# Hawk-Conformer-MoE step: separate SBUF for the bias tables, loaded and split during the convolution

## The chip, the cores and the metric

The kernel runs on one core of a Trainium2 chip. The metric is the time of one execution on the device in microseconds. The core has five engines that run side by side, each with its own instruction queue, and that wait for each other through semaphores: TensorE (PE: matmuls and transposes), VectorE (DVE), ScalarE (ACT), GpSimd (POOL) and SyncE (SP, which here only issues DMAs). They work on SBUF and PSUM; DMA queues move data between HBM and SBUF.

## The reference, cut to what matters

One inference step of a one-layer decoder for 256 prompt tokens and 8 x 4 sample tokens (288 in all), model width 1024:

```python
hn = rmsnorm(x, g_mix)
z = hn @ w_in                       # xa | u_glu (2 x 1024) | gate_a | gate_b
xa_c = causal_dwconv(xa, ..., w_conv_a, b_conv_a)      # width 4
y_a = rglru(xa_c, ...)
v = u_glu[..., :D] * sigmoid(u_glu[..., D:])
v_c = causal_dwconv(v, ..., w_conf_dw, b_conf_dw)      # width 31
y_b = silu(layernorm(v_c, ...)) @ w_conf_pw + b_conf_pw
h = x + (sigmoid(gate_a) * y_a + sigmoid(gate_b) * y_b) @ w_out
# mixture of experts on rmsnorm(h, g_ffn): top 4 of 32
for e in range(32):
    g = minimum(xf @ w_gate[e] + b_gate[e], 7)
    u = clip(xf @ w_up[e] + b_up[e], -7, 7)
    hdn = (u + 1) * (g * sigmoid(1.702 * g))
    out += combine[:, e] * (hdn @ w_down[e] + b_down[e])
y = rmsnorm(h + out, g_final)
```

The 32 experts' weights (3 x 4 MB each) are read once. The change touches the three tables `b_gate`, `b_up` and `b_down`, 32 rows of 1024 float32 each.

## The kernel before, in words

The program has a mixer stage (all before the experts) and an expert stage. It is written with explicit waits, so each engine's order is the order of the code.

**Mixer.** The 1024 channels stand in 8 tiles of 128 partitions, each with 256 prompt columns and 32 sample columns. PE computes the products with `w_in` tile by tile (L846), ACT empties them, and POOL multiplies value and sigmoid for each tile (L519, L521). The width-31 convolution runs on DVE, two tiles at a time, in a loop of four turns over pairs of tiles: each turn has 31 taps on two tiles, the first tap of a turn as a tensor_scalar (L1348) and the others as scalar_tensor_tensor of 128x256 float32 with two tensor inputs in SBUF (L1351), 60 in a turn. The sample columns go another way: POOL multiplies them with all taps (L535, eight instructions for two tiles, written into `taps_s`), and half way through a turn, after the first 30 taps, DVE reduces them (L1335, L1339). That releases POOL to write the products for the next pair of tiles. So POOL is half a turn ahead of DVE. After the loop DVE starts the width-4 convolution (L1320, L1323) and subtracts the mean (L1357); POOL adds up the tiles (L563) for the mean, a matmul with ones on PE (L906), and then, from ACT's squares (L690), for the variance (L568, PE L911). Layer norm, the RG-LRU scan (L1393), the pointwise matmul (L928) and the merge (L1398, L1401) follow.

**From the merge to the first gather.** PE multiplies with `w_out` (L985 for the 32 sample tokens, L951 for the two prompt tiles); DVE adds the residual (L1410, L1415); ACT sums squares (L632); DVE scales (L1419). The normed rows `h_tok` are then cut into three bf16 parts, since the gather is a bf16 matmul with a 0/1 selection: ACT casts (L737), POOL subtracts the cast from the rest (L601, function `rest`), ACT casts again, twice per token tile, tiles in the order 2, 0, 1. PE turns the rows (L829) and computes router logits (L978), DVE takes the top four (L1435 to L1446), PE ranks the tokens (L1006), DVE writes the selection (L1474), and PE gathers the first expert's inputs (L1020, L1022). `keep_warm` (L959) are idle matmuls of PE on the identity.

**The bias tables.** A bias enters the experts' matmuls as a bf16 matmul whose weights pick three rows of a table: the float32 bias as three bf16 parts on partitions 0 to 95. `bias` is that table for gate, up and down. `load_bias(m)` (L575) issues three DMAs of 32 rows each from POOL's queue. `split_bias(m)` makes the parts on POOL: a cast (L583), a subtraction (L590), a cast, a subtraction, a cast, each waiting for the one before. Before the change `bias` and its raw rows lie in the work area `ws` on top of the mixer's tiles, so POOL waits for the merge (`s_m`), issues the loads, clears the unused rows (L606, and L607 for `h_rows`, the parts of the sample rows), and then splits between the calls of `rest`:

```python
                pool.wait_ge(s_m, NT)
                load_bias(0)
                load_bias(1)
                pool.memset(bias[3 * E:, :, :], 0.0)
                pool.memset(h_rows[3 * T_S:, :], 0.0)
                split_bias(0)
                pool.wait_ge(s_btab, 1)
                load_bias(2)
                rest(0, TILE_ORDER[0])
                split_bias(1)
                rest(1, TILE_ORDER[1])
                rest(2, TILE_ORDER[2])
                split_bias(2)
```

PE waits before the first gather for all h parts (`s_split`, 9 casts) and for the tables of gate and up (`s_btab` 2).

**Experts.** SP streams chunks of 2 MB into a ring of six slots; the chunk `m` waits until PE has used chunk `m-6` (`used`). The first of these waits stands behind PE's first chunk of expert products (L1042), after the first gather.

Of the kernel before, what the change touches and what calls it, by code (L numbers as in the profile page):

```python
# [22 lines left out]
BF16 = mybir.dt.bfloat16  # L23
# [3 lines left out]
P = 128  # L27
D = 1024
NT = D // P
# [8 lines left out]
E = 32  # L38
CAP = 64
# [55 lines left out]
def build(nc, A, O):  # L95
    with ExitStack() as ctx:
        def sb(name, shape, dt=F32):
            return ctx.enter_context(nc.sbuf_tensor(name, shape, dt))

        def sem(name):  # L100
            return ctx.enter_context(nc.semaphore(name))
# [13 lines left out]
        bias_rows = sb("bias_rows", [P, E], BF16)  # L115
        tri = sb("tri", [P, P], BF16)
# [19 lines left out]
        def take(words):  # L136
            at[0] += words
            assert at[0] <= WS, at
            return ws[:, at[0] - words:at[0]]
# [34 lines left out]
        stc_rows = ig_w[:, 0:2 * D].rearrange("p (h d) -> p h d", h=2)  # L174
        st_v = ga_w[:, TW:TW + 2 * D].rearrange("p (b d) -> p b d", b=2)
# [20 lines left out]
        x_e_w = take(2 * NT * CAP)  # L196
        x_e = x_e_w.rearrange("p (b k s) -> p b k s", b=2, k=NT)
# [4 lines left out]
        bias = take(3 * D // 2).bitcast(BF16).rearrange("p (m d) -> p m d", m=3)  # L202
        raw_bias = [y_e, x_e_w, y_e]
# [26 lines left out]
        s_btab = sem("bias_tables_ready")  # L230
        s_gfin = sem("g_final_loaded")
# [145 lines left out]
        with nc.Block() as block:  # L377
# [113 lines left out]
            def _(pool):  # L491
# [4 lines left out]
                pool.memset(ones_h[:], 1.0).then_inc(s_const, 1)  # L496
                pool.wait_ge(s_seed, 1)
# [12 lines left out]
                for name, r, n in (("w_conf_dw", W_DW, KC), ("w_conv_a", W_CA, KA), ("b_conv_a", B_CA, 1),  # L510
                                   ("b_rg_a", B_RA, 1), ("b_rg_x", B_RX, 1), ("rg_lambda", LAM, 1), ("b_conf_dw", B_DW, 1),
                                   ("g_conf_ln", G_LN, 1), ("b_conf_ln", B_LN, 1), ("b_conf_pw", B_PW, 1)):
                    pool.dma_start(par_rows[r:r + n, :], A[name][0] if n > 1 else A[name]).then_inc(s_par, 16)

                for c in range(0, NT, 2):
# [14 lines left out]
                    for cc in (c, c + 1):  # L530
                        pool.wait_ge(s_v, 2 * cc + 2)
                        v = vx[:, cc, HC + T_P:].rearrange("p (s t) -> p s t", s=SEQS)
                        w = par[:, cc, W_DW:W_DW + KC].unsqueeze(1).to_broadcast([P, SEQS, KC])
                        for t in range(STEPS):
                            ins = pool.tensor_tensor(taps_s[:, cc % 2, :, t, :], v[:, :, t:t + KC], w, ALU.mult)  # L535
                        ins.then_inc(s_tap, 1)

# [35 lines left out]
                def load_bias(m):  # L573
                    for r in range(3):
                        pool.dma_start(raw_bias[m][r * E:(r + 1) * E, :],  # L575
                                       A[("b_gate", "b_up", "b_down")[m]][0]).then_inc(s_bias[m], 16)

                def split_bias(m):

                    pool.wait_ge(s_bias[m], 48)  # L580
                    for s in range(3):
                        n = (3 - s) * E
                        ins = pool.tensor_copy(bias[0:n, m, :], raw_bias[m][0:n, :])  # L583
                        if s == 2:
                            ins.then_inc(s_btab, 1)
                            break
                        ins.then_inc(s_part, 1)
                        pool.wait_ge(s_part, 4 * m + 2 * s + 1)
                        n -= E
                        pool.tensor_tensor(raw_bias[m][0:n, :], raw_bias[m][0:n, :], bias[0:n, m, :],  # L590
                                           ALU.subtract).then_inc(s_part, 1)
                        pool.wait_ge(s_part, 4 * m + 2 * s + 2)

# [10 lines left out]
                load_bias(0)  # L604
                load_bias(1)
                pool.memset(bias[3 * E:, :, :], 0.0)  # L606
                pool.memset(h_rows[3 * T_S:, :], 0.0)  # L607
                split_bias(0)
                pool.wait_ge(s_btab, 1)
                load_bias(2)  # L610
                rest(0, TILE_ORDER[0])
                split_bias(1)
                rest(1, TILE_ORDER[1])
                rest(2, TILE_ORDER[2])
                split_bias(2)
# [5 lines left out]
            def _(act):  # L621
# [149 lines left out]
                act.wait_ge(s_btab, 3)  # L771
# [43 lines left out]
            def _(pe):  # L815
# [328 lines left out]
                pe.wait_ge(s_btab, 2)  # L1144
# [21 lines left out]
                pe.wait_ge(s_btab, 3)  # L1166
# [72 lines left out]
            def _(dve):  # L1239
# [157 lines left out]
                for c in range(NT):  # L1397
                    V.scalar_tensor_tensor(mt[:, c, :], full(f"pw{c}")[:, 0:T], par[:, c, B_PW:B_PW + 1], gate_b[:, c, :],  # L1398
                                           ALU.add, ALU.mult).then_inc(empt_v, 1)
                    dve.wait_ge(empt_v, EV(f"pw{c}"))  # L1400
                    V.tensor_tensor(mt[:, c, :], mt[:, c, :], gate_a[:, c, :], ALU.add).then_inc(s_m, 1)  # L1401
                gain = g_ffn[:, :].unsqueeze(2).to_broadcast([P, NT, P])
# [250 lines left out]
```

## Time and profile before

| | us |
|---|---|
| median of 3 runs | 1261.91 (1260.13 to 1262.08) |
| the profiled execution | 1262.29 |
| its span | 1260.2 |
| from the span's start to the first convolution tap on DVE | 40.6 |
| convolution loop on DVE | 40.6 to 168.6 |
| merge done | 244.6 |
| first gather on PE | 305.2 |
| first expert products on PE | 310.3 |

PE is busy 94% of the span, DVE 42%, ACT 14%, POOL 9%. From some 345 us to the end the DMA queues move 420 GB/s, the experts' weights. The stretches before that are told apart by which engine waits for which.

### The profile page before, as it was taken

To read this page: it belongs to the slowest core of one execution; us is meant where nothing else is said; L and a number is where in the kernel's file an instruction comes from. 1 tells how busy PE (TensorE), PEld (TensorE's weight loads), DVE (VectorE), ACT (ScalarE), POOL (GpSimd) and SP (SyncE) were. 2 spreads that over 40 slices of the span, in tenths; PEclk is the share of its full clock that TensorE was granted. 3 is DMA by queue.
4 is the path that set the end of the run, shared out by engine and by line. 5 is a ranking of instruction groups with operands and counts; after the bars stand their busy time and mean duration, and the time that the engine had idled before them with its cause. 6 is when DMAs were issued, how large, how long until landed. Compare 5 with 4: busy or idle time off the path is not lost.

```text
span 1260.2 us, 18031 instructions
## 1 busy us (share of the span) xinstructions
PE 1188.1 (94%) x6801; PEld 591.1 (47%) x6802; DVE 524.8 (42%) x1001; ACT 179.1 (14%) x325; POOL 109.4 (9%) x134
## 2 busy tenths in 40 slices
PE   6999959988999999999999999999999999999996
PEld 4777747646444444444444443434343443434532
DVE  2799996845233232322323233323232323223242
ACT  3211217113010101010110101010101010101102
POOL 2422430174000000000000000000000000000000
PEclk9999979988999999999999999999999999999999
DMA  9943403355999999999999999999999999999991
GB/s 290 337 158 134 167 30 143 117 188 186 388 411 422 421 420 422 422 422 422 422 422 421 422 422 421 423 422 422 422 422 422 422 423 421 422 422 420 422 415 48
DMA packets 84661, 440.34 MB, mean 349 GB/s; under 512 B 8079, under 2 KB 30735, under 8 KB 35715
## 3 DMA queue, kind: packets, MB, share of 16 engines
q1 hardware_dynamic: 83075, 436.71, 85.8%
q0 software_dynamic: 1408, 3.14, 0.8%
q8 instruction: 25, 0.41, 0.1%
q14 instruction: 9, 0.07, 0.0%
q10 hardware_dynamic: 144, 0.00, 0.0%
HBM read 438.24 MB, written 2.43 MB: 350 GB/s over the span
## 4 chain that ended last, share of the span: by engine, by line
PE 59%; DMA 18%; DVE 10%; issue 7%; ACT 3%; POOL 1%; DVEq 1%; SPq 0%; ACTq 0%; POOLq 0%
PE ps L1042 28%; DMA ring<-in_w_up 17%; PE ps L1101 12%; PE ps L1020 6%; PE ps L1126 5%; DVE ws L1351 4%; PE ps L829 3%; PE ps L1022 1%; DMA ws<-in_b_gate 1%; PE ps L846 1%; PE ps L1033 1%; DVEq L1350 1%; PE ps L1130 1%; DVE ws L1323 1%; PE ps L951 1%
## 5 line engine op out<-in xcount | busy, mean ns | idle before, releaser
L1042 PE MATMUL ps<-ring,ws 128*64 128x512 f32 x2032 | 455.5, 596 | 18.5 <-DMA ring<-in_w_up 18.1
L1042 PEld LDWEIGHTS ps<-ring,ws 128*64 128x64 f32 x2032 | 138.6, 137 | 306.5 <-issue 263.5
L1101 PE MATMUL ps<-ring,ws 128*64 128x512 f32 x992 | 220.3, 597 | 0.0
L1506 DVE TENSOR_SCALAR ws<-ps 64x1024 f32<-64x1024 f32 x32 | 38.9, 1216 | 294.6 <-PE ps L1042 294.6
L846 PE MATMUL ps<-ws,ring 128*128 128x288 f32 x640 | 160.6, 415 | 0.7 <-issue 0.7
L846 PEld LDWEIGHTS ps<-ws,ring 128*128 128x128 f32 x640 | 124.7, 195 | 35.6 <-issue 0.8
L1101 PEld LDWEIGHTS ps<-ring,ws 128*64 128x64 f32 x992 | 70.0, 138 | 128.6 <-issue 126.2
L1527 DVE TENSOR_TENSOR acc<-ps,acc 128x1024 f32<-128x1024 f32 x32 | 39.2, 1225 | 194.1 <-PE ps L1126 194.1
L1020 PE MATMUL ps<-ws 128*128 128x64 bf16 x1536 | 112.2, 226 | 3.6 <-DVE ws L1474 3.6
L1351 DVE SCALAR_TENSOR_TENSOR ws<-ws,par x240 | 113.6, 551 | 0.0
L1020 PEld LDWEIGHTS ps<-ws 128*128 128x128 bf16 x1536 | 108.8, 166 | 6.7 <-issue 4.7
L764 ACT COPY ws<-ps 64x512 f32<-64x512 f32 x64 | 37.1, 579 | 289.0 <-PE ps L1101 288.6
L829 PE MATMUL ps<-ident,ws 64*128 64x64 f32 (+9 forms) x424 | 61.6, 287 | 15.4 <-DVE ws L1277 10.0
L1493 DVE TENSOR_TENSOR ws<-ps,g_ffn_c 128x512 f32<-128x512 f32 x32 | 22.1, 692 | 122.0 <-PE ps L1022 122.0
L829 PEld LDWEIGHTS ps<-ident,ws 64*128 64x128 f32 (+9 forms) x424 | 49.5, 178 | 49.8 <-issue 47.1
L1126 PE MATMUL ps<-ws 128*128 128x512 f32 x128 | 63.2, 618 | 1.5 <-ACT ws L764 1.5
L745 ACT COPY ws<-ps 128x512 f32<-128x512 f32 x32 | 18.7, 586 | 300.7 <-PE ps L829 300.7
L1022 PE MATMUL ps<-ws 128*128 128x64 bf16 x256 | 57.8, 226 | 0.0
L1532 DVE TENSOR_TENSOR acc<-ps,acc 32x256 f32<-32x256 f32 x64 | 26.7, 418 | 43.9 <-PE ps L1130 43.2
L1022 PEld LDWEIGHTS ps<-ws 128*128 128x128 bf16 x256 | 42.6, 166 | 0.0
L1126 PEld LDWEIGHTS ps<-ws 128*128 128x128 f32 x128 | 21.8, 189 | 42.4 <-issue 42.4
L755 ACT COPY ws<-ps 128x384 f32<-128x384 f32 x16 | 7.7, 478 | 227.9 <-PE ps L829 227.9
(202 smaller groups left out, 758.7 us busy)
## 6 DMA issues: line engine op xcount, KB each, us to landing
ring<-in_w_gate SPq DMA_DIRECT2D x127, 1024.0 KB, 20.9
ring<-in_w_up SPq DMA_DIRECT2D x127, 1024.0 KB, 23.3
ring<-in_w_down SPq DMA_DIRECT2D x124, 1024.0 KB, 19.3
ring<-in_w_in SPq DMA_DIRECT2D x20, 1024.0 KB, 11.2
ring<-in_w_conf_pw SPq DMA_DIRECT2D x4, 1024.0 KB, 6.3
ring<-in_w_out SPq DMA_DIRECT2D x4, 1024.0 KB, 6.8
ws<-in_w_down SPq DMA_DIRECT2D x2, 1024.0 KB, 5.8
acc<-in_x_prompt SPq DMA_DIRECT2D x2, 512.0 KB, 4.0
```

The lines of the kernel that those rows point to most:

```text
L764: ins = act.copy(y_e[d * CAP:(d + 1) * CAP, h * 512:(h + 1) * 512], ps[h * CAP:(h + 1) * CAP, bk, :])
L829: return nc.tensor.transpose(dst, src, ident[0:k, 0:k])
L846: ins = nc.tensor.matmul(z[:, 0:T], w[:, k, i * P:(i + 1) * P], hn[:, k, :], start=(k == 0), stop=(k == NT - 1))
L1020: nc.tensor.matmul(z, h_split[:, s, i, t::NT], sel[:, b, i, :], start=(s == 0 and i == 0), stop=False)
L1022: ins = nc.tensor.matmul(z, h_rows[:, t::NT], sel[:, b, 2, :], start=False, stop=True)
L1042: ins = nc.tensor.matmul(ps[m * CAP:(m + 1) * CAP, bk + h, :], x_e[:, b, 2 * q + t, :], w[:, m, t, h * 512:(h + 1) * 512], start=False, st ...
L1101: ins = nc.tensor.matmul(ps[h * CAP:(h + 1) * CAP, bk, :], hid_t[:, b, k, :], w[:, h * 512:(h + 1) * 512], start=False, stop=(k == NT - 1))
L1126: ins = nc.tensor.matmul(ps[:, bk + h, :], sel_t[0:rows, i * P:(i + 1) * P], y_e[0:rows, h * 512:(h + 1) * 512], start=True, stop=True)
L1351: V.scalar_tensor_tensor(y, x, w, y, ALU.mult, ALU.add).then_inc(s_conv, 1)
L1506: V.tensor_scalar(g_e, pair_ps(0, k), LIMIT, None, ALU.min).then_inc(s_gc, 1)
L1527: ins = V.tensor_tensor(acc[:, i, :], ps[:, bk:bk + 2, :].rearrange("p h n -> p (h n)"), acc[:, i, :], ALU.add)
L1532: ins = V.tensor_tensor(a, ps[c * T_S:(c + 1) * T_S, bk, 0:256], a, ALU.add)
```

## The change

- `bias` becomes a tensor of its own in SBUF (128 x 3 x 1024 bf16), no longer laid over the mixer's tiles. POOL clears all of it near the start of the program, after `ones_h` and ahead of the steps on `ident` and `tri` and of the parameter loads.
- The raw rows of the tables lie in the area of `ig_w`, which is free during the convolution: gate and down in its first 1024 columns, up in the next.
- `load_bias(0)` and `load_bias(1)` stand on POOL after the tap products of the first pair of tiles; `split_bias(0)` and `load_bias(2)` after those of the second, `split_bias(1)` after the third, `split_bias(2)` after the fourth.
- After the merge POOL only runs the three calls of `rest`. The clearing of the unused rows of `h_rows` moves to DVE, with a semaphore `s_zrow` for which PE's first gather waits.
- PE waits for all three tables before the first gather. ACT's wait and PE's second wait for them are gone.
- The reserve for descriptors of POOL's DMAs is set to 8192 bytes.

```diff
@@ constants, POOL @@
                 pool.memset(ones_h[:], 1.0).then_inc(s_const, 1)
+                pool.memset(bias[:, :, :], 0.0)
                 pool.wait_ge(s_seed, 1)
@@ convolution loop, POOL @@
                         ins.then_inc(s_tap, 1)
+                    if c == 0:
+                        load_bias(0)
+                        load_bias(1)
+                    else:
+                        split_bias(c // 2 - 1)
+                    if c == 2:
+                        pool.wait_ge(s_btab, 1)
+                        load_bias(2)
@@ after the merge, POOL @@
                 pool.wait_ge(s_m, NT)
-                load_bias(0)
-                load_bias(1)
-                pool.memset(bias[3 * E:, :, :], 0.0)
-                pool.memset(h_rows[3 * T_S:, :], 0.0)
-                split_bias(0)
-                pool.wait_ge(s_btab, 1)
-                load_bias(2)
-                rest(0, TILE_ORDER[0])
-                split_bias(1)
-                rest(1, TILE_ORDER[1])
-                rest(2, TILE_ORDER[2])
-                split_bias(2)
+                for n, i in enumerate(TILE_ORDER):
+                    rest(n, i)
@@ after the merge, DVE @@
+                dve.wait_ge(s_m, NT)
+                V.memset(h_rows[3 * T_S:, :], 0.0).then_inc(s_zrow, 1)
@@ before the first gather, PE @@
                 pe.wait_ge(s_split, 3 * TILES)
-                pe.wait_ge(s_btab, 2)
+                pe.wait_ge(s_btab, 3)
+                pe.wait_ge(s_zrow, 1)
                 gather(0, 0)
@@ program @@
-    nc = bacc.Bacc("TRN2", target_bir_lowering=False, num_devices=1)
+    nc = bacc.Bacc("TRN2", target_bir_lowering=False, num_devices=1, dynamic_dma_scratch_size=8192)
```

On POOL, in the second turn of its loop (tiles 2 and 3), the tap products were followed by the products of the next pair of tiles:

```order
L535 TENSOR_TENSOR ws<-ws,par 128x8x31 [waits v_ready]
L535 TENSOR_TENSOR ws<-ws,par 128x8x31 x3
L519 TENSOR_TENSOR ws<-ws 128x256 [waits psum_emptied_by_scalar]
L521 TENSOR_TENSOR ws<-ws 128x8x4
L519 TENSOR_TENSOR ws<-ws 128x256 [waits psum_emptied_by_scalar]
L521 TENSOR_TENSOR ws<-ws 128x8x4
L535 TENSOR_TENSOR ws<-ws,par 128x8x31 [waits v_ready,conf_conv_steps]
```

Now, at the same place on POOL (L557 is the former L535, L541 the former L519):

```order
L557 TENSOR_TENSOR ws<-ws,par 128x8x31 x3
L526 CAST bias<-ws 96x1024 [waits gate_bias_loaded]
L533 TENSOR_TENSOR ws<-ws,bias 64x1024 [waits bias_parts_steps]
L526 CAST bias<-ws 64x1024 [waits bias_parts_steps]
L533 TENSOR_TENSOR ws<-ws,bias 32x1024 [waits bias_parts_steps]
L526 CAST bias<-ws 32x1024 [waits bias_parts_steps]
L518 DMA ws<-in_b_down 32x1024 [waits bias_tables_ready]
L518 DMA ws<-in_b_down 32x1024 x2
L541 TENSOR_TENSOR ws<-ws 128x256 [waits psum_emptied_by_scalar]
```

Five instructions of 1024 columns and three DMA issues have come between; the third and fourth turns get the same five without the DMAs.

On POOL after the merge, before: the first two subtractions of `rest` (L601) stood behind the loads, the clearing and the whole first split:

```order
L606 MEMSET ws 32x3072
L607 MEMSET ws 32x1024
L583 CAST ws<-ws 96x1024 [waits gate_bias_loaded]
L590 TENSOR_TENSOR ws<-ws 64x1024 [waits bias_parts_steps]
L583 CAST ws<-ws 64x1024 [waits bias_parts_steps]
L590 TENSOR_TENSOR ws<-ws 32x1024 [waits bias_parts_steps]
L583 CAST ws<-ws 32x1024 [waits bias_parts_steps]
L575 DMA ws<-in_b_down 32x1024 [waits bias_tables_ready]
L575 DMA ws<-in_b_down 32x1024 x2
L601 TENSOR_TENSOR ws<-ws 64x1024 [waits h_parts_cast,psum_filled]
```

And now, on POOL after the merge, from the last output DMA to the load of `g_final`:

```order
L601 DMA out<-ws 8x1024
L610 TENSOR_TENSOR ws<-ws 64x1024 [waits h_parts_cast,psum_filled,merged_ready]
L610 TENSOR_TENSOR ws<-ws 32x1024 [waits h_parts_cast]
L610 TENSOR_TENSOR ws<-ws 128x1024 [waits h_parts_cast,psum_filled]
L610 TENSOR_TENSOR ws<-ws 128x1024 [waits h_parts_cast]
L610 TENSOR_TENSOR ws<-ws 128x1024 [waits h_parts_cast,psum_filled]
L610 TENSOR_TENSOR ws<-ws 128x1024 [waits h_parts_cast]
L616 DMA ws<-in_g_final 128x1024 [waits psum_filled]
```

Nothing but the six subtractions is left there.

## Rows read from the trace of the kernel before

**Rows 1.** Chain of waits (start us, us, engine and line)

```profile
267.88 2.14 POOL ws L601
```

**Rows 2.** Waits of PE over the span (us in total, times, longest)

```profile
PE ps L1042 <- DMA ring<-in_w_up: 18.1, 17, 1.3
PE ps L906 <- POOL ws L563: 15.8, 1, 15.8
```

**Rows 3.** Timeline, PE, 265 to 311 us (start us, us, instruction, count, [idle before <-releaser])

```profile
265.26 7.11 PE L951 MATMUL ps<-ring,ws 128*128 128x512 f32 x16
277.23 1.94 PE L829 MATMUL ps<-ident,ws 128*128 128x128 f32 x8 [4.85 <-DVE lg L1435]
278.96 8.42 PE L951 MATMUL ps<-ring,ws 128*128 128x512 f32 x16
...
298.71 2.83 PE L959 MATMUL ps<-ident 128*128 128x128 f32 x12
305.17 0.55 PE L1020 MATMUL ps<-ws 128*128 128x64 bf16 x6 [3.63 <-DVE ws L1474]
```

**Rows 4.** Timeline, POOL, 252 to 304 us

```profile
252.60 0.95 POOL L607 MEMSET ws<- 32x1024 bf16 x1
...
303.93 1.04 POOL L583 CAST ws<-ws 32x1024 bf16<-32x1024 f32 x1
```

**Rows 5.** Timeline, DVE, 252 to 306 us

```profile
252.16 1.94 DVE L1419 TENSOR_SCALAR ws<-acc,stat 128x1024 f32<-128x1024 f32 x1
...
263.76 0.69 DVE L1415 TENSOR_TENSOR acc<-ps,acc 128x512 f32<-128x512 f32 x1 [6.03 <-PE ps L951]
...
289.95 0.75 DVE L1419 TENSOR_SCALAR ws<-acc,stat 128x1024 f32<-128x1024 f32 x1
...
299.19 1.45 DVE L1466 TENSOR_SCALAR rank<-rank 128x96 f32<-128x96 f32 x1
...
301.92 3.10 DVE L1474 TENSOR_SCALAR ws<-slot_no,rank 128x64 bf16<-128x64 f32 x3
...
305.05 0.57 DVE L1474 TENSOR_SCALAR ws<-slot_no,rank 128x64 bf16<-128x64 f32 x3
```

**Rows 6.** Timeline, DVE: tap runs of turn 1 (second half), 2 and 4 (first half)

```profile
58.18 17.05 DVE L1351 SCALAR_TENSOR_TENSOR ws<-ws,par  x32
...
76.24 11.17 DVE L1351 SCALAR_TENSOR_TENSOR ws<-ws,par  x28
...
139.51 13.86 DVE L1351 SCALAR_TENSOR_TENSOR ws<-ws,par  x28
```

**Rows 7.** Windows of POOL (stretch, us, busy us (count), clock, DMA share, GB/s)

```profile
76.24:87.41 11.17, 0.00 (x0) 1.00 0.17 48
...
58.18:75.23 17.05, 9.28 (x12) 1.00 0.69 222
```

**Rows 8.** Timeline, POOL: a product beside an idle DVE, sums beside the taps

```profile
28.46 0.63 POOL L519 TENSOR_TENSOR ws<-ws 128x256 f32<-128x256 f32 x1 [20.01 <-ACT ws L660]
...
139.71 4.67 POOL L563 TENSOR_TENSOR ws<-ws 128x288 f32<-128x288 f32 x5
```

**Rows 9.** Lines by form, POOL: groups of the split (busy us, mean ns | idle before)

```profile
L590 POOL TENSOR_TENSOR ws<-ws 64x1024 f32<-64x1024 f32 x3 | 6.3, 2115 | 0.2
...
L583 POOL CAST ws<-ws 96x1024 bf16<-96x1024 f32 x3 | 3.1, 1030 | 4.9 <-DMA ws<-in_b_gate 4.9
...
L606 POOL MEMSET ws<- 32x3072 bf16 x1 | 2.7, 2653 | 0.0
```

**Rows 10.** Timeline, SP's DMA issues, 235 to 330 us

```profile
313.96 0.33 SPq L426 DMA_DIRECT2D ring<-in_w_gate  x1
```

**Rows 11.** Timeline, all engines, 0 to 12 us

```profile
1.08 0.91 DVE L1253 MEMSET acc<- 128x1024 f32 x1 [0.96 <-PEq L1643]
...
2.02 0.34 SPq L384 DMA_DIRECT2D acc<-in_x_sample  x1
...
7.27 1.04 ACT L632 ACTIVATE ws<-acc 128x1024 f32<-128x1024 f32 x1
```

## What the change does to the time, told before it was run

> **What bounds the kernel now.** PE is busy 94% of the span, so a share tells little; I went stage by stage and asked what ends last. From the first expert products on, PE and the weight stream pass the bound between them: all of PE's waits for weights there come to 18.1 us [rows 2]. That stage begins with the first gather. The chunk that starts the lasting stream is issued at 313.96, behind PE's first chunk of products [rows 10]. Whatever moves the first gather moves all behind it by as much, so the question is when the gather starts: 305.17 now [rows 3].
>
> Two stretches before it matter. After the merge, the chain goes through the load of `b_gate` and POOL's splitting, and reaches `rest` only at 267.88 [rows 1]. Before that, DVE's convolution is the bound: from 40.6 to 168.6 us DVE runs taps, turn after turn, and PE then stands 15.8 us waiting for the last sums [rows 2]. PE, ACT and POOL have room there; DVE has none. So the change takes work out of one stretch that is on the path and puts it on POOL beside another one that is on the path, and all depends on whether DVE feels it.
>
> **What is gained after the merge.** (a) `rest` for tile 2 no longer waits for the split. It needs the turned rows, there at about 256.9, so it starts 11 us earlier than 267.88. Then other work is late: the next square on ACT needs PE's `out01`, and the DVE addition after that starts at 263.76 and takes 0.69 [rows 5]. From there the chain takes square, root and scaling, by an estimate 2.6 us, so tile 0 is normed at about 267, with 5 us to spare: PE is in L951 until 272.4, and turns at once instead of at 277.23 after a wait of 4.85 [rows 3]: 4.9 us. L951 behind the turn takes 7.1, as the one at 265.26 does, instead of 8.42 [rows 3], since PE no longer stands still ahead of it: 1.3 us; and for the turn of 1.94 itself I take 0.8 off for the same reason, an estimate. Together **7.0 us**.
>
> (b) At the end of the stretch DVE is held up by POOL. The first selection (three tensor_scalar of 64 columns) takes 3.10 us from 301.92, and the same three take 0.57 at 305.05; the first ends at 305.02, within 0.1 us of the end of POOL's last cast at 304.97 [rows 4, 5]. The split of `down` behind `rest` holds three steps on mask and ranks ahead of it as well, the longest of them 1.45 us for 96 columns [rows 5], 3.0 us in all by my estimate. Without it the selection would be ready 5.5 us earlier relative to PE's last logits. The idle matmuls ahead of the gather are then the last: they end 298.71 + 2.83 = 301.54 now [rows 3], and start 0.8 us earlier and run mostly at the higher clock. I take **5.2 us**, between 3.9 (as long as now) and 5.5.
>
> (c) DVE's new clearing of `h_rows` costs nothing: DVE stands 4.0 us after the merge waiting for PE's first residual, and POOL's clearing of the same rows took 0.95 [rows 4]. If that cover were gone it would cost up to 0.9. POOL's clearing no longer holds DVE's scaling at 252.16, which takes 1.94 beside it and 0.75 alone [rows 5]; PE's `out00` hides that, so I count nothing. Gain in all 7.0 + 5.2 = **12.2 us**, bounds 10.9 and 12.9.
>
> **What is paid in the convolution.** POOL gets 15 more instructions of 1024 columns: 9 casts of 1.03 and 6 subtractions of 2.12 us [rows 9], 9.3 + 12.7 = 22.0 us. All fall in second halves of DVE's turns 1 to 3. POOL itself has room: it is half a turn ahead (about 16 us), and a split with its loads takes about 10.5 at this pace. PE waits longer for the new columns (some 20 us where it had nothing to do later but wait 15.8), and still has its five products done before the sums are.
>
> What DVE feels is read from its taps. With POOL idle, 28 taps take 11.17 us, 0.40 each [rows 6, 7]. Beside five of POOL's sums of 288 columns they take 13.86 [rows 6, 8]: 2.69 more, 0.54 for each. In the second half of turn 1, 32 taps take 17.05 instead of 12.77: 4.28 more, beside 12 instructions of POOL, eight of 248, two of 256 and two of 32 columns [rows 6, 7]. At 0.41 to 0.43 for each of the ten long ones that is it. A product of 256 columns alone takes 0.63 [rows 8], one of 288 would take 0.69. So each instruction of POOL costs DVE its own duration less 0.15 to 0.2, at every size that the trace has. By this rule a subtraction costs 1.92 and a cast 0.83: 6 x 1.92 + 9 x 0.83 = 11.5 + 7.5 = **19.0 us**; with 0.15 it is 19.7. The trace has no 1024-column instruction of POOL beside such a tap, so this goes four times beyond the longest row. The nearest rows at that length are DVE's operations on one SBUF input, which wait out POOL's whole instructions: the scaling at 252.16 ends 0.55 us after POOL's clearing has ended at 253.55 [rows 4, 5]. This is why I take the full length.
>
> The Trainium skill, SBUF — State Buffer, "SBUF: two separate sides", has a rule that speaks against this change: VectorE and GpSimd share a port pair under an exclusive lock, held for the whole instruction, against a VectorE operation in a two-port mode or with two SBUF inputs. By that rule the price is the 19 us; by a split of the bandwidth, which the page denies, it would be the 14.3 of the second rival. The rows on short instructions agree with either.
>
> **At the start.** POOL's clearing covers 3072 columns, 2.65 us [rows 9], ahead of `ident` and the parameter loads. `ident` is then ready at about 5.5, PE needs it at 10. The parameters land 2.65 later, which moves SP's second chunk from 13.9 to 16.6; PE needs it at 38. Nothing. But DVE's first clearing (1.08, 0.91 us) is such an operation as waits for POOL, and SP's load of the sample tokens at 2.02 waits for it [rows 11]. It could start only at about 4, so that load goes out at 4.6. It now lands by 6.7, behind the prompt; at 4.6 the queues are free of that, and by an estimate it takes 2.8 us and is there at 7.4, against ACT's third square at 7.27 [rows 11]. I take **0.3 us**, bounds 0 and 2.1 (if it takes as long again).
>
> **The DMAs.** Moved loads: 1.2 MB, at 420 GB/s some 3 us of all queues, beside a w_in stream that is tens of us ahead of PE. Nine issues of 0.5 us on POOL fall into its room. The second reserve of descriptors is halved or so; I have no row for a full one and count nothing, with up to 5 us of POOL's room as the bound.
>
> **Sum.** 19.0 + 0.3 - 12.2 = +7.1 us on the profiled execution of 1262.3, so 1269.4 there; the median of the runs is 0.4 lower, **1269.0**.
>
> **Rivals.**
> - *The forecast*, POOL's instructions hold the taps for their full length: 17.5 to 20.5, plus 0 to 2.1, less 12.9 to 10.9: +4.6 to +11.7, 1266.5 to 1273.6. Chance 0.70.
> - *Turns.* Both engines take every other slot while they collide. A tap streams 256 columns, 0.27 of its 0.40 us. It then takes 0.67, in which POOL gets 0.27 + 0.13 = 0.40 done, so each us of POOL costs 0.65: 22.0 x 0.65 = 14.3, sum +2.4, 1264.3. For it: the rows up to 288 columns fit it within 0.1. Against: the one-input rows above. Chance 0.10.
> - *Casts pass.* Only instructions of POOL with two inputs hold the taps: 11.5, sum -0.4, 1261.5. For it: all the rows beside taps that I count are products and sums. Against: even a clearing, which reads nothing, holds DVE's scaling [rows 4, 5]. Chance 0.06.
> - *The hold is per instruction, not per length* (the other side: faster). DVE loses one slot of arbitration, about 0.5 us, for each of POOL's instructions however long: 15 x 0.5 = 7.5, sum -4.4, 1257.5. For it: the trace shows only 0.41 to 0.54 at each. Against: the three sizes rise with length, 0.41, 0.43, 0.54. It decides from a mean hold under 0.8 us (12.2 / 15). Chance 0.07.
> - *The convolution is hidden*, or the order of POOL shifts so that the splits fall elsewhere: -11.9, 1250.0. Against it stands PE's wait of 15.8 for the sums [rows 2]. Chance 0.02.
> - *A starved POOL* (descriptors, or its half turn of lead used up), 5 us more than the forecast, near 1274. Chance 0.05.
>
> **How the numbers follow.** A measurement of this kernel can tell about 0.2%, 2.5 us, from no change. Slower by more: the forecast, the starved POOL and half of the turns, 0.80. Within: the other half and most of the casts, 0.10. Faster: 0.10. The range takes in the forecast and the turns: 1264 to 1273.6; widened to 1263.5.
>
> **What would show it.** Taps (L1351) whose longest instance is about 2.4 us instead of about 1, and second halves of turns 1 to 3 that are each about 6.3 us longer; POOL's subtractions beside them stretched little; PE's wait for L906 still there; PE turning tile 0 without a wait; the first selection in about 0.6 us. Measured from the merge to the first gather the time should fall from 60.5 to about 48.3 us, and from the start to the merge rise from 244.6 to about 264. It is wrong if the merge comes at about 252 (the per-instruction hold), or if the last third of the way to the gather keeps its 3.1 us selection.

## The result: 0.6% slower, as forecast

| | before | after |
|---|---|---|
| median of 5 runs, us | 1261.91 (1260.13 to 1262.96) | 1269.34 (1266.99 to 1271.23) |
| the profiled execution | 1262.29 | 1267.2 |
| start to first tap | 40.6 | 39.9 |
| convolution loop | 127.9 | 147.6 |
| loop end to merge | 76.1 | 76.1 |
| merge to first gather | 60.6 | 47.5 |
| first gather to first expert products | 5.1 | 4.9 |

The ratio of the medians is 1.0058, with an interval of 1.0045 to 1.0071. The forecast was 1269.0 in 1263.5 to 1273.6. The two profiled executions differ by 4.9 us, the medians by 7.4. The stages from the start to the first products (310.31 before, 315.99 after) come to +5.7 (-0.7 + 19.7 + 0.0 - 13.1 - 0.2, with rounding); what lies behind the first products took 0.8 us less in the profiled run of after. The five runs of this kernel lie up to 4.2 us apart, and the profiled one, 1267.2, is among the two shortest; where the others lose more was not followed.

The page of the kernel after, its span and busy times (us, share, instructions), and from section 5 the group of the taps (busy us, mean ns of one, idle time before):

```profile
span 1265.2 us, 18031 instructions
...
PE 1182.9 (93%) x6801; PEld 587.6 (46%) x6802; DVE 533.8 (42%) x1002; ACT 179.7 (14%) x325; POOL 109.6 (9%) x133
...
L1349 DVE SCALAR_TENSOR_TENSOR ws<-ws,par x240 | 133.8, 634 | 0.0
```

The shares hardly moved: PE 93% where it was 94%, POOL 9% as before. A reader who compares only them would see nothing of the 20 us lost and 13 won. The mean of a tap, 634 ns, hides it as well, since most taps are as short as ever. The view of this line's instructions shows minimum, median and maximum in ns:

```profile
L1349 DVE SCALAR_TENSOR_TENSOR ws<-ws,par x240: 471/479/2344, 40.9 to 187.1; - x120
```

The timeline of DVE after (start us, us, instruction, count) shows where the long ones are. Lines 1, 3, 4 are the second halves of turns 1 to 3; line 2 is the first half of turn 2, line 5 that of turn 4:

```profile
57.93 23.73 DVE L1349 SCALAR_TENSOR_TENSOR ws<-ws,par  x32
...
82.68 11.17 DVE L1349 SCALAR_TENSOR_TENSOR ws<-ws,par  x28
...
96.32 23.50 DVE L1349 SCALAR_TENSOR_TENSOR ws<-ws,par  x32
...
134.44 22.51 DVE L1349 SCALAR_TENSOR_TENSOR ws<-ws,par  x32
...
157.92 14.42 DVE L1349 SCALAR_TENSOR_TENSOR ws<-ws,par  x28
```

The first halves of turns 2 and 3, with POOL idle, are the 11.17 of [rows 6] to the hundredth. The second half of turn 1 went from 17.05 [rows 6] to 23.73, those of turns 2 and 3 from 16.98 and 16.56 to 23.50 and 22.51: 19.2 us in all. The rest of the 19.7 is in the first halves of turn 1 (14.08 to 14.55) and turn 4 (13.86 to 14.42), less 0.5 at turn 4's first tap. POOL stands beside them like this (timeline, POOL, the first split):

```profile
64.62 1.23 POOL L526 CAST bias<-ws 96x1024 bf16<-96x1024 f32 x1
65.93 2.18 POOL L533 TENSOR_TENSOR ws<-ws,bias 64x1024 f32<-64x1024 f32 x1
68.17 1.11 POOL L526 CAST bias<-ws 64x1024 bf16<-64x1024 f32 x1
69.37 2.18 POOL L533 TENSOR_TENSOR ws<-ws,bias 32x1024 f32<-32x1024 f32 x1
71.61 1.11 POOL L526 CAST bias<-ws 32x1024 bf16<-32x1024 f32 x1
...
275.55 2.12 POOL L610 TENSOR_TENSOR ws<-ws 64x1024 f32<-64x1024 f32 x1 [9.53 <-PE ps L827]
...
306.59 2.12 POOL L610 TENSOR_TENSOR ws<-ws 128x1024 f32<-128x1024 f32 x1 [1.16 <-ACT ws L736]
```

POOL's five take the lengths of [rows 9] plus 0.06 to 0.2: POOL is hardly stretched, DVE bears it all. The last two lines are the first and last subtraction of `rest` after the merge, alone with what they wait for: PE's turn and ACT's cast.

After the merge, PE (timeline; 283.82 is the product ahead of the turn of tile 0, which stands at 265.26 in [rows 3]):

```profile
283.82 7.11 PE L949 MATMUL ps<-ring,ws 128*128 128x512 f32 x16
290.77 1.05 PE L827 MATMUL ps<-ident,ws 128*128 128x128 f32 x8
291.65 7.03 PE L949 MATMUL ps<-ring,ws 128*128 128x512 f32 x16
...
309.26 1.58 PE L957 MATMUL ps<-ident 128*128 128x128 f32 x12
311.10 0.54 PE L1018 MATMUL ps<-ws 128*128 128x64 bf16 x6 [0.26 <-DVE ws L1474]
```

The turn has no wait before it, where 4.85 stood; the gather waits 0.26 where it waited 3.63. DVE in the same stretch (timeline; the scaling of tile 0, one step on the ranks, the first selection):

```profile
284.84 0.75 DVE L1419 TENSOR_SCALAR ws<-acc,stat 128x1024 f32<-128x1024 f32 x1
...
309.74 0.21 DVE L1466 TENSOR_SCALAR rank<-rank 128x96 f32<-128x96 f32 x1
...
310.37 0.58 DVE L1474 TENSOR_SCALAR ws<-slot_no,rank 128x64 bf16<-128x64 f32 x3
```

The scaling is through 5.2 us before PE turns; the selection is 0.58 instead of 3.10, the step on the ranks 0.21 instead of 1.45 [rows 5]. And PE's waits (us in all, times, longest), which answer to [rows 2]:

```profile
PE ps L827 <- issue: 19.7, 1, 19.7
PE ps L1040 <- DMA ring<-in_w_up: 19.4, 19, 1.3
PE ps L904 <- POOL ws L593: 14.1, 1, 14.1
```

The wait for the last sums of the convolution is still there, 14.1 after 15.8: the loop is still the bound of its stretch, so what it lost is lost. For the new 19.7 us the view names no releaser; they end at 150.82, 0.1 us after POOL's two copies of new columns, which stand behind the last split. Since PE then still waits 14.1 for the sums, they cost nothing by themselves.

### The profile page after: what moved, and what is told of

It reads as the page before. It is cut to its first block, busy times and chain, and to the rows that moved or that the text cites. A ratio compares the mean times of both kernels' runs of the same rounds, so it can differ in the third digit from the quotient of the medians.

```text
span 1265.2 us, 18031 instructions
## 1 busy us (share of the span) xinstructions
PE 1182.9 (93%) x6801; PEld 587.6 (46%) x6802; DVE 533.8 (42%) x1002; ACT 179.7 (14%) x325; POOL 109.6 (9%) x133
## 4 chain that ended last, share of the span: by engine, by line
PE 59%; DMA 19%; DVE 9%; issue 8%; ACT 2%; DVEq 1%; SPq 0%; POOL 0%; ACTq 0%; POOLq 0%
PE ps L1040 27%; DMA ring<-in_w_up 19%; PE ps L1099 12%; PE ps L1018 5%; PE ps L1124 5%; DVE ws L1349 4%; PE ps L827 3%; PE ps L949 2%; PE ps L1020 1%; PE ps L844 1%; PE ps L1031 1%; DVEq L1348 1%; PE ps L1128 1%; DVE ws L1321 1%; PE ps L1092 1%
## 5 line engine op out<-in xcount | busy, mean ns | idle before, releaser
L1040 PE MATMUL ps<-ring,ws 128*64 128x512 f32 x2032 | 455.7, 595 | 19.7 <-DMA ring<-in_w_up 19.4
L1349 DVE SCALAR_TENSOR_TENSOR ws<-ws,par x240 | 133.8, 634 | 0.0
L827 PE MATMUL ps<-ident,ws 64*128 64x64 f32 (+9 forms) x424 | 62.1, 288 | 30.1 <-issue 19.7
L1124 PEld LDWEIGHTS ps<-ws 128*128 128x128 f32 x128 | 21.8, 189 | 42.5 <-issue 42.5
## 6 DMA issues: line engine op xcount, KB each, us to landing
ring<-in_w_down SPq DMA_DIRECT2D x124, 1024.0 KB, 19.7
```

The costliest lines, as they stand in the source:

```text
L827: return nc.tensor.transpose(dst, src, ident[0:k, 0:k])
L1040: ins = nc.tensor.matmul(ps[m * CAP:(m + 1) * CAP, bk + h, :], x_e[:, b, 2 * q + t, :], w[:, m, t, h * 512:(h + 1) * 512], start=False, st ...
L1124: ins = nc.tensor.matmul(ps[:, bk + h, :], sel_t[0:rows, i * P:(i + 1) * P], y_e[0:rows, h * 512:(h + 1) * 512], start=True, stop=True)
L1349: V.scalar_tensor_tensor(y, x, w, y, ALU.mult, ALU.add).then_inc(s_conv, 1)
```

## The experiments

The theory: the loss is POOL's arithmetic alone, one instruction after the other, each holding DVE's taps for its length less 0.15 to 0.2 us; the gain after the merge is two things that can be had without that price. Rivals: shared slots, casts that pass, a hold per instruction, or a loss that comes from the loads and the changed order and not from the arithmetic. Ratios are against the kernel before, run on the same chip beside them (its medians: 1261.27, 1261.82 and 1261.47 us). Stages (us, from the profiled executions):

| kernel | loop | loop end to merge | merge to gather | longest tap | median |
|---|---|---|---|---|---|
| before | 127.9 | 76.1 | 60.6 | 1.02 | 1261.9 |
| a_again | 147.5 | 76.1 | 47.5 | 2.34 | 1269.4 |
| c_none | 128.2 | 76.1 | 47.5 | 1.23 | 1248.9 |
| c_casts | 136.5 | 77.8 | 47.5 | 2.07 | 1258.4 |
| c_subs | 140.1 | 77.8 | 47.5 | 2.34 | 1261.9 |
| b_late | 127.9 | 76.1 | 55.1 | 1.02 | 1257.2 |
| v_slots | 127.9 | 76.1 | 47.5 | 1.02 | 1250.9 |
| v_slots2 | 127.9 | 76.1 | 47.5 | 1.01 | 1249.1 |
| v_clear | 127.9 | 76.1 | 47.5 | 1.02 | 1251.0 |
| c_clears | 125.3 | 76.1 | 47.5 | 1.02 | 1245.4 |
| c_clear1 | 129.3 | 77.8 | 47.5 | 1.75 | 1251.5 |

### The change once more

No edit: the kernel after.

> The changed kernel once more, nothing edited. Its profiled run was 4.9 us above that of before, its median of five 7.4 us above. Theory (the sum: +19.7 in the convolution, -13.0 from merge to gather): a new profile again shows these two terms within 0.3 us, and the time is +5.5 to +9 us on before. Rival (the terms themselves scatter from run to run): the convolution loop differs from 147.6 us by over 1 us, or the stretch from merge to first gather from 47.5 by over 1 us.

Ratio 1.0062 [1.0049, 1.0075], all stages within 0.2 us of the first profile. The result stands.

### The change without the splitting

```diff
@@ split_bias(m) of the kernel after @@
                     pool.wait_ge(s_bias[m], 48)
-                    for s in range(3):
-                    ...
+                    pool.memset(bias[:, m, 0:2], 0.0).then_inc(s_btab, 1)
```

> The changed kernel with the arithmetic of the three splits left out (no casts, no subtractions; the bias tables stay zero, so the biases are not added); loads, the early clearing and everything after the merge as in the changed kernel. Theory (the full-length hold of DVE's taps is the whole loss): the convolution loop takes 127.5 to 128.5 us as before, the merge-to-gather stretch keeps its 47.5, and the time is 12 to 14 us below before, some 1249. Rival (the loads from POOL's queue or the early clearing cost something too): the loop stays 2 us or more above 128, or the first tap comes later than 41, and the time is above 1251.

Ratio 0.9905 [0.9891, 0.9920]; the loop takes 128.2. This kernel keeps the loads, their nine issues and the waits of POOL for them, and leaves out the parts of the bias. What it keeps comes to 0.3 us; the other 19.3 of the 19.7 us are the fifteen instructions. DVE's second halves of turns 1 and 2 (timeline):

```profile
58.15 17.37 DVE L1338 SCALAR_TENSOR_TENSOR ws<-ws,par  x32
...
90.17 16.99 DVE L1338 SCALAR_TENSOR_TENSOR ws<-ws,par  x32
```

### Casts alone, and subtractions alone

Casts alone (the subtractions left out):

```diff
@@ split_bias(m) of the kernel after @@
                         ins.then_inc(s_part, 1)
-                        pool.wait_ge(s_part, 4 * m + 2 * s + 1)
-                        n -= E
-                        pool.tensor_tensor(raw_bias[m][0:n, :], raw_bias[m][0:n, :], bias[0:n, m, :],
-                                           ALU.subtract).then_inc(s_part, 1)
-                        pool.wait_ge(s_part, 4 * m + 2 * s + 2)
+                        pool.wait_ge(s_part, 2 * m + s + 1)
```

> The changed kernel with the six subtractions of the splits left out, the nine casts kept (the bias tables then hold the rounded bias three times over, so biases are wrong). Theory (a cast, with one input and one output in SBUF, holds a tap for its duration less 0.15 to 0.2): 9 x 0.83 to 0.88, the convolution loop is 7.5 to 8 us above 127.9, time 5 us below before, some 1257. Rival (only two-input instructions of POOL hold the taps): the loop is at 128 to 129 us, time some 1249.

Subtractions alone (the casts left out):

```diff
@@ split_bias(m) of the kernel after @@
-                    for s in range(3):
-                        n = (3 - s) * E
-                        ins = pool.tensor_copy(bias[0:n, m, :], raw_bias[m][0:n, :])
-                        ...
+                    for s in range(2):
+                        n = (2 - s) * E
+                        pool.tensor_tensor(raw_bias[m][0:n, :], raw_bias[m][0:n, :], bias[0:n, m, :],
+                                           ALU.subtract).then_inc(s_part, 1)
+                        pool.wait_ge(s_part, 2 * m + s + 1)
+                    pool.memset(bias[:, m, 0:2], 0.0).then_inc(s_btab, 1)
```

> The changed kernel with the nine casts left out and the six subtractions kept (a clearing of 2 columns stands in for the last step; the tables stay zero, so biases are not added). Theory: 6 x 1.92 to 1.97 = 11.5 to 11.8 us, the convolution loop at about 139.5, time 1 us below before, some 1261. Rival (a long subtraction and the taps share by turns, and the rest of the loss came from the casts): 8 us or less, loop below 136.

c_casts: 0.9973 [0.9964, 0.9983]. c_subs: 1.0003 [0.9994, 1.0013]. The timeline of DVE in c_casts (turns 1 and 2), then that in c_subs (turn 1):

```profile
58.32 20.13 DVE L1345 SCALAR_TENSOR_TENSOR ws<-ws,par  x32
...
93.10 19.77 DVE L1345 SCALAR_TENSOR_TENSOR ws<-ws,par  x32
```

```profile
58.03 21.20 DVE L1343 SCALAR_TENSOR_TENSOR ws<-ws,par  x32
```

Against the 17.37 of c_none three casts add 2.76, 0.92 each, and two subtractions 3.83, 1.92 each. Over the whole loop it is (136.5 - 128.2) / 9 = 0.92 for a cast of 1.03 us and (140.1 - 128.2) / 6 = 1.97 for a subtraction of 2.12 (from the unrounded times). By loop or by turn, both are the instruction's length less 0.1 to 0.2. That settles it against three rivals: casts that pass would add nothing, a hold per instruction would give a cast and a subtraction the same price, and shared slots would give 0.67 and 1.38. The parts alone add up to 8.3 + 11.8 = 20.1, together they cost 19.3.

In both kernels loop end to merge rose by 1.7 us as well, which no expectation had; their medians are 1.2 us further above that of c_none than their loops say, their ratios 0.3 to 0.6 us. The timeline of PE in c_casts shows it, with the granted clock in windows (stretch, us, PE busy us (count), clock as a share of 2.4 GHz, DMA share, GB/s) below; the last fence has PE's matmuls ahead of the same wait in c_none:

```profile
179.94 12.78 PE L840 MATMUL ps<-ws,ring 128*128 128x288 f32 x48
194.85 0.72 PE L905 MATMUL ps<-ws,ones 128*128 128x288 f32 x2 [2.14 <-POOL ws L594]
195.41 17.37 PE L840 MATMUL ps<-ws,ring 128*128 128x288 f32 x64
```

```profile
193.00:195.00 2.00, 0.15 (x1) 1.00 0.63 164
195.00:197.00 2.00, 2.00 (x6) 0.64 0.99 418
197.00:199.00 2.00, 2.00 (x5) 0.51 1.03 438
199.00:205.00 6.00, 6.00 (x26) 1.00 0.04 12
```

```profile
171.47 13.56 PE L833 MATMUL ps<-ws,ring 128*128 128x288 f32 x48
```

PE waited 2.14 us for the variance sum, and the clock stood at the lower of its two levels, 1.2 GHz, from about 195.5 to 199; the 64 matmuls took 17.37 us. In c_none the wait was 1.36 and the same 64 took 15.68. In the kernels before and after it was 1.0. The sum itself is no later: the matmul that uses it starts 16.0 us after the one for the mean in c_casts (178.82 to 194.85) as in c_none (170.35 to 186.40). PE is only done sooner with the 48 matmuls between them, 12.78 us instead of 13.56 in c_none and 13.95 before, since the clock behind the mean's matmul is back at 2.4 GHz by about 182 (PE began at 178.82), in c_none only at about 175 (PE began at 170.35). c_subs and c_clear1 are alike: 12.67 and 12.82 for the 48, then waits of 2.25 and 2.11. So PE gains under 1 us ahead of the wait and loses 1.7 behind it. Why the clock comes back sooner in these three is open.

### The kernel before, with the last split behind the gather

```diff
@@ the kernel before, POOL after the merge @@
                 rest(2, TILE_ORDER[2])
+                pool.wait_ge(s_xg, 1)
                 split_bias(2)
```

> The kernel before with one part of the gain alone: the split of the down table waits until the first gather is done, so it no longer runs beside DVE's ranks and first selection; tables, areas and loads stay where they were. Theory (that split alone holds DVE, term b of the sum): the first selection takes 0.6 instead of 3.1 us, the first gather starts 5.0 to 5.6 us earlier, the time is 5 us below before, some 1257. Rival (the hold comes from the subtraction of the last token tile, or the idle matmuls end last as before): 0 to 2.5 us, 1260 to 1262.

Ratio 0.9969 [0.9957, 0.9981]: 3.9 us faster with one line. From the merge to the gather it is 55.1 instead of 60.6. DVE's first selection (timeline of DVE):

```profile
298.40 0.58 DVE L1475 TENSOR_SCALAR ws<-slot_no,rank 128x64 bf16<-128x64 f32 x3
```

It comes at 298.4, and POOL's first cast of that split at 302.74. So part (b) of the gain, put at 5.2, is 5.4, measured alone: from the end of the last product with `w_out` to the gather it is 12.6 instead of 18.0. The part up to that end is nearly untouched here (42.5 for 42.6), so the two are separate, and the rest of the 13.05 is (a).

### All of the gain, without the price

The splits go to places where POOL is idle and DVE has nothing of the path: gate behind the variance sums, up between the calls of `rest`, down behind the first gather.

```diff
@@ from the kernel after; raw rows in the areas of hn_w (gate), x_e_w (up), y_e (down) @@
-                    if c == 0:
-                        load_bias(0)
-                        load_bias(1)
-                    else:
-                        split_bias(c // 2 - 1)
-                    if c == 2:
-                        ...
@@ POOL behind the variance sums @@
+                pool.wait_ge(filled, JOB["gb7"] + 1)
+                load_bias(0)
+                split_bias(0)
@@ POOL after the merge @@
                 pool.wait_ge(s_m, NT)
-                for n, i in enumerate(TILE_ORDER):
-                    rest(n, i)
+                load_bias(1)
+                load_bias(2)
+                rest(0, TILE_ORDER[0])
+                split_bias(1)
+                rest(1, TILE_ORDER[1])
+                rest(2, TILE_ORDER[2])
+                pool.wait_ge(s_xg, 1)
+                split_bias(2)
```

PE again waits for two tables ahead of the first gather and for the third behind it, and ACT has its wait back, as in the kernel before.

> The changed kernel, but with the three splits in stretches where POOL is idle and DVE is idle or has room: gate after the last use of the normed input (its raw rows lie there), beside ACT's exponentials; up between the subtractions of token tile 2 and of tile 0; down behind the first gather. Raw rows of up and down lie where they did before the change. Theory: the convolution loop is back at 128 us and the stretch from merge to first gather stays at 47.5, so 1249 to 1250, 12 to 13.5 us below before. Rival (the split only moves its hold to other operations of DVE on the path, such as the product ahead of the scan or the scaling of tile 0): the loss shows up between the loop's end and the merge (76.1 us now) or in the merge-to-gather stretch, 3 to 7 us, so 1253 to 1257.

> The version with the splits in free slots once more, beside the one with the moved clearing: stages as in its first profile (loop 127.9, merge to gather 47.5), time 11 to 12.5 us below before.

Ratios 0.9917 [0.9902, 0.9931] and, once more, 0.9906 [0.9892, 0.9920]: 10 to 12 us faster than the kernel before, about 19 faster than the change. The loop is back at 127.9 and the gather stays at 47.5 after the merge: the same 22 us of arithmetic on POOL lengthened no stage here. The first median lies 2 us above that of c_none, the second with it. The timeline of POOL and the one of DVE show the only meeting with a long instruction of DVE:

```profile
210.59 1.03 POOL L528 CAST bias<-ws 64x1024 bf16<-64x1024 f32 x1
211.70 4.32 POOL L535 TENSOR_TENSOR ws<-ws,bias 32x1024 f32<-32x1024 f32 x1
```

```profile
211.47 2.57 DVE L1382 TENSOR_TENSOR ws<-ws 128x2304 f32<-128x2304 f32 x1 [4.36 <-ACT ws L709]
```

DVE's instruction began first and took its 2.57; POOL's subtraction took 4.32 instead of 2.12: 2.2 more, and until DVE ends at 214.04 there are 2.34. So the hold works both ways, and here whoever came second waited.

### Clearings in place of the arithmetic

Do instructions of POOL that only write hold the taps? First, five clearings of the same width where each split's five instructions stood:

```diff
@@ split_bias(m) of the kernel after @@
-                        ins = pool.tensor_copy(bias[0:n, m, :], raw_bias[m][0:n, :])
-                        ...
+                    for s in range(5):
+                        ins = pool.memset(bias[0:3 * E, m, :], 0.0)
+                        ...
```

> The changed kernel with each split's five steps replaced by five clearings of the same table, 96 x 1024 bf16, about 0.95 us each: POOL writes SBUF but reads nothing (tables stay zero, so biases are not added). Theory A (any instruction of POOL holds the taps): 15 x 0.75 = 11 us, loop at 139, time some 1260. Theory B (what is held is the reading side, so clearings pass beside taps with two inputs, as DVE's own clearing at the start passed beside POOL's of 2.67 us): loop at 128 to 129, time some 1249.

Ratio 0.9869 [0.9853, 0.9885], the fastest kernel of all, although it leaves nothing out of the loop that c_none has. DVE (turn 2), then POOL beside it (timelines):

```profile
90.75 16.14 DVE L1344 SCALAR_TENSOR_TENSOR ws<-ws,par  x32
```

```profile
97.45 4.96 POOL L525 MEMSET bias<- 96x1024 bf16 x5
102.38 5.01 POOL L536 TENSOR_TENSOR ws<-ws 128x256 f32<-128x256 f32 x1
107.35 0.30 POOL L538 TENSOR_TENSOR ws<-ws 128x32 f32<-128x32 f32 x1
```

Five clearings of 0.99 run beside the taps, and the taps take less than the 16.99 of c_none. What is new is the product of 256 columns behind them: 5.01 us for 0.65 to 0.9. It ends at 107.4, just after DVE's run of taps has ended at 106.9. Now it is POOL that is kept out, for a whole row of taps. DVE's run is 0.85 shorter than in c_none, and the first tap of turn 3 behind it 0.55 longer (1.36 for 0.81). Half of the 2.9 us by which this loop is shorter than that of c_none stands in turn 4, where POOL's five sums of 288 columns come late (148.32, 6.62 us) and are kept out too: the first half takes 11.17 for 13.85, the second 13.83 for 12.76.

The Trainium skill, SBUF — State Buffer, "SBUF: two separate sides", says that the lock works against a VectorE operation with two SBUF inputs only where GpSimd's operation reads SBUF. The trace agrees for the clearings, which the taps did not feel.

To see whether a single clearing does this to the product, in the fast version the clearing of `bias` near the start moved into the loop, one table per turn (v_clear), and in the kernel after one clearing took each split's place (c_clear1):

```diff
@@ v_clear, from v_slots @@
-                pool.memset(bias[:, :, :], 0.0)
...
                         ins.then_inc(s_tap, 1)
+                    if c:
+                        pool.memset(bias[:, c // 2 - 1, :], 0.0).then_inc(s_part, 1)
```

> The version with the splits in free slots, with the clearing of the bias tables moved from the start into the convolution: one table (128 x 1024 bf16) after the tap products of turns 2, 3 and 4 on POOL. With five such clearings (96 rows) in each turn the convolution loop had come out at 125.3 us, 3.0 below the 128.3 without them, because POOL's products of 256 columns behind them waited for a gap of DVE (3.2 and 5.0 us instead of 0.65 and 0.78) and DVE's taps ran at full pace meanwhile. Theory A (one clearing is enough to bring POOL's next reading instruction behind DVE): loop at 125.3 to 126.5, time 1.5 to 2.5 us below the version without it, some 1248.5. Theory B (it took five in a row, or was a matter of when they ended): loop at 127.9, same time as that version.

```diff
@@ c_clear1, split_bias(m) of the kernel after @@
                     pool.wait_ge(s_bias[m], 48)
-                    for s in range(3):
-                    ...
+                    pool.memset(bias[0:3 * E, m, :], 0.0).then_inc(s_btab, 1)
```

> The changed kernel with each split's five steps replaced by one clearing of 96 x 1024 bf16 (tables stay zero, so biases are not added); with five clearings the loop took 125.3 us, with only 2 columns cleared 128.3. Theory A (one long write-only instruction is enough): the products or the copy behind it last over 2 us and the loop is at 125.3 to 126.5. Theory B: loop at 128, products of 0.65 to 0.9 us.

v_clear: 0.9923 [0.9909, 0.9938], c_clear1: 0.9918 [0.9903, 0.9933]. POOL in v_clear (timeline):

```profile
96.58 0.95 POOL L561 MEMSET bias<- 128x1024 bf16 x1
97.49 0.72 POOL L542 TENSOR_TENSOR ws<-ws 128x256 f32<-128x256 f32 x1
```

One clearing does not keep the product out, 0.72, and the loop is 127.9 and 129.3 (why c_clear1's is 1.0 above that of c_none, with a longest tap of 1.75, was not followed). So v_clear is no gain over v_slots. No kernel can use c_clears as it stands, since it wins by clearing a table that is then empty.

The clearings need not be the cause. In the kernel before, which has none in the loop, POOL (first) met the taps of turn 1's first half (second) like this:

```profile
54.77 1.52 POOL L519 TENSOR_TENSOR ws<-ws 128x256 f32<-128x256 f32 x1 [6.48 <-ACT ws L660]
```

```profile
41.62 14.08 DVE L1351 SCALAR_TENSOR_TENSOR ws<-ws,par  x28
```

The product took 1.52 for 0.63 and ended at 56.3, 0.6 after the run of taps; in the kernel after, the same product took 1.99. In all twelve profiles (before, after and the ten runs), every reading instruction of POOL that came 4.4 us or more after both POOL's last reading one and the start of the run of taps waited for the end of the run, 16 in all. Every one that came 4.2 us or less after one of the two got in beside the taps (the product at 70.29 before: 4.22 idle, 1.09 us). Five clearings fill 4.96 us, one fills 0.95. So the pause in POOL's reading may be what counts; no run had such a pause made on purpose, and this stays argued.

## Why the prediction was right, step by step

- **The price in the convolution**, 19.0 by the rule, bounds 17.5 to 20.5: 19.7, of which 19.3 belong to the fifteen instructions. The rule held four times beyond the longest row it was read from. Of its two constants, length less 0.15 was the better: it gives 19.7. Measured apart, a cast costs 0.92 (0.83 predicted) and a subtraction 1.97 (1.92). The second halves got 6.7, 6.5 and 6.0 longer for the 6.3 told, and the longest tap is 2.344 us for 2.4. The step that mattered was to go by instructions on one SBUF input that wait out POOL's whole length [rows 4, 5], and not by the rows up to 288 columns, which also fit shared slots. The row named for it was no model for the taps, though: the scaling at 252.16 waits for a clearing, and clearings do not hold taps (c_clears). The better row was the first selection, which ends with POOL's last cast. So the length was rightly read, from a pair of instructions that behaves otherwise.
- **(a) up to the last product with `w_out`**, 7.0: 7.7. From the start of L951 to the turn it is 6.95 instead of 11.97 (5.0, told 4.9), the turn 0.88 instead of 1.73 (0.85, told 0.8), L951 behind it 7.03 instead of 8.42 (1.4, told 1.3), and PE reaches that L951 0.4 us earlier after the merge, which was not in the sum.
- **(b) the last third of the way**, 5.2: 5.4 in the kernel after, 5.4 alone in b_late. Parts (a) and (b) together, 13.05, lie just above the bounds that were told, 10.9 to 12.9. The gather now waits 0.26 for the selection: the idle matmuls, told to be last, end at 310.84, the first selection at 310.95.
- **(c) DVE's clearing of `h_rows`** costs nothing: it takes 0.48 at 263.75, and DVE waits 3.35 behind it for PE.
- **The start**, +0.3: this step had a wrong mechanism. The rows of after (timeline, all engines):

```profile
1.08 0.91 DVE L1251 MEMSET acc<- 128x1024 f32 x1 [0.95 <-PEq L1643]
...
1.35 2.67 POOL L497 MEMSET bias<- 128x3072 bf16 x1
...
2.02 0.34 SPq L384 DMA_DIRECT2D acc<-in_x_sample  x1
...
2.23 0.07 DVE L1254 MEMSET lg<- 128x12 f32 x1
```

  DVE's clearing did not wait for POOL's, nor did its small ones that began in the middle of it; the sample load went out at 2.02 as before [rows 11]. The step took a clearing for an operation like the scaling at 252.16, which has an SBUF input and did wait. The price of this is 0, not 0.3. The first tap comes between 39.9 and 41.3 in all the runs, in no order with the edits, which is more than the step was about.
- **The experts** start 5.9 us later in the trace (gather 305.17, now 311.10), the first chunk of the lasting stream 5.7 later, and PE's waits for weights are 19.4 for 18.1: all behind the gather moved with it, as told.

The sum by measured terms is 19.67 - 13.05 = +6.6 us, for +7.1 told and +7.4 between the medians. Each of the two large terms was told 0.7 to 0.9 us too small, and these two errors cancel almost wholly. That the sum is so near is luck in part; with either error alone it would still have been inside the range. What lies between the +6.6 and the +7.4 is not in the sum: the start (-0.7), the stretch to the first products (-0.2) and what lies behind them (-0.8) go the other way in the profiled runs, and the medians differ by 2.5 us more than these two runs.

Where the expectations of the experiments missed: c_casts (told 1257, 1258.4) and c_subs (told 1261, 1261.9), where the 1.7 us of the longer wait and the lower clock behind it were not expected; b_late (told 5 us below before, 3.9); v_slots (told 12 to 13.5 below before, 10.4 by its ratio, and 11.9 the second time), although its stages came as told; c_clears (told a loop of 128 and some 1249, 125.3 and 1245.4); v_clear, where theory A (1248.5) failed and the loop stayed at 127.9; c_clear1 (loop told at 128, 129.3).

## What to carry to other kernels

An idle share of POOL is no free room while DVE runs operations on two SBUF inputs back to back and is the bound: a reading instruction of POOL that gets in costs DVE nearly its full length, at all the lengths measured here, 248 to 1024 columns. Move such work to where DVE waits for another engine, and look for POOL's long instructions beside short DVE steps just ahead of a stage's end; here one wait of POOL gave 3.9 us, and the right places for all three splits gave 10 to 12. Before giving a busy stretch more work, look at what still waits for its end: the 15.8 us wait of PE said at once that nothing of the price would be hidden.

## What the runs showed of the hardware that was not expected

- The hold between POOL and DVE works in both directions: a subtraction of POOL took 4.32 us instead of 2.12 behind DVE's 2.57 us instruction, while taps waited out POOL's subtractions (2.34 instead of 0.48).
- POOL's clearings hold neither taps nor DVE's clearings, but they did hold DVE's scaling (1.94 us for 0.75 [rows 5]). After five in a row POOL's next product waited for the end of DVE's taps (5.01 us for 0.72), after one it did not. The same wait stands in kernels without clearings wherever POOL had read nothing for 4.4 us or more beside a run of taps, and nowhere at 4.2 or less. The cause is open.
- A wait of 2.14 us on PE was followed by about 3.5 us at 1.2 GHz and cost 1.7 us in the 64 matmuls behind it, where one of 1.36 cost nothing. Three kernels that differ from c_none only in POOL's instructions met it, all three after PE had been done sooner with the matmuls ahead.
